# Seven block products for the up pair too, in the last feed-forward block of a decoder step

## The reference

```python
def swiglu(h, w_gate, w_up, w_down):
    return (jax.nn.silu(h @ w_gate) * (h @ w_up)) @ w_down
...
h = modulate(rms_norm(x, norm_ffn2[i]), sh3, sc3)
x = x + 0.5 * gt3[:, None, :] * swiglu(h, ffn2_gate[i], ffn2_up[i], ffn2_down[i])
```

## Time and profile before

| | |
|---|---|
| median of 3 runs | 1440.79 us (1439.36 to 1442.4) |
| the profiled execution | 1442.35 us, span 1440.7 us |
| busy, share of the span | PE 97%, DVE 68%, ACT 37%, POOL 5% |
| granted TensorE clock, mean | 0.990 |
| group 1 of the last feed-forward block, four turns | 1158 to 1244 us of the span |
| group 2, four turns | 1290 to 1377 us |

### The profile page before, as it was taken

How to read it: one execution, slowest core, us unless ns; L and a number is a source line. 1 busy time by engine, 2 the same in 40 slices (tenths; PEclk the granted TensorE clock), 3 DMA queues, 4 the chain that set the end, 5 groups by cost and what they waited for, 6 DMA issues and landing times.

```text
span 1440.7 us, 28804 instructions
## 1 busy us (share of the span) xinstructions
PE 1391.4 (97%) x11790; PEld 1346.0 (93%) x11790; DVE 976.9 (68%) x1731; ACT 539.3 (37%) x797; POOL 77.4 (5%) x118
## 2 busy tenths in 40 slices
PE   6999999999999999999999998999999999999996
PEld 5899999999998999999899897999899999999996
DVE  5446775357546588998998997854554786456745
ACT  5323343224336222524233236422342344224433
POOL 6100000010001000000000000000000000000000
PEclk8999999999999999999999999999999999999998
DMA  9754646455364223213334443626312242223221
GB/s 323 229 180 146 210 150 205 146 166 146 97 206 143 87 88 93 89 60 103 128 123 147 147 156 126 212 89 199 110 41 91 74 134 89 96 81 117 90 87 60
DMA packets 132701, 189.49 MB, mean 132 GB/s; under 512 B 4621, under 2 KB 112545, under 8 KB 132386
## 3 DMA queue, kind: packets, MB, share of 16 engines
q1 hardware_dynamic: 111388, 112.54, 24.7%
q0 software_dynamic: 17136, 66.87, 13.8%
q10 hardware_dynamic: 4070, 8.57, 1.6%
HBM read 173.73 MB, written 15.18 MB: 131 GB/s over the span
## 4 chain that ended last, share of the span: by engine, by line
PE 82%; DVE 11%; ACT 3%; DMA 2%; issue 2%; POOL 0%; DVEq 0%; ACTq 0%; POOLq 0%
PE pu L642 47%; PE pu L817 13%; PE pu L806 11%; PE pu L658 3%; PE pg L679 2%; DVE w_lo L1667 2%; DMA work<-in_w_ada 1%; ACT w_hi L1214 1%; PE pg L1052 1%; DVE d L2087 1%; PE pg L715 1%; PE pg L1116 1%; DMA raw_a<-in_w_ada 1%; DVE w_lo L1956 1%; DVE work L2197 1%
## 5 line engine op out<-in xcount | busy, mean ns | idle before, releaser
L1667 DVE TENSOR_TENSOR w_lo<-raw,w_hi 128x1024 fp32r<-128x1024 f32 x152 | 186.1, 1225 | 259.2 <-ACT w_hi L1214 259.0
L1214 ACT CAST w_hi<-raw 128x1024 fp32r<-128x1024 f32 x152 | 158.8, 1046 | 402.0 <-PE pu L642 360.6
L642 PE MATMUL pu<-h_hi,w_hi 128*128 128x260 f32 x1408 | 288.5, 286 | 5.2 <-DVE w_lo L1667 3.6
L642 PE MATMUL pu<-h_hi,w_lo 128*128 128x260 f32 x1408 | 284.0, 283 | 0.0
L642 PE MATMUL pu<-h_lo,w_hi 128*128 128x260 f32 x1408 | 283.6, 283 | 0.0
L642 PEld LDWEIGHTS pu<-h_hi,w_hi 128*128 128x128 f32 x1408 | 217.5, 189 | 9.0 <-DVE w_lo L1667 5.3
L642 PEld LDWEIGHTS pu<-h_lo,w_hi 128*128 128x128 f32 x1408 | 217.4, 189 | 0.0
L642 PEld LDWEIGHTS pu<-h_hi,w_lo 128*128 128x128 f32 x1408 | 217.4, 189 | 0.0
L2087 DVE SCALAR_TENSOR_TENSOR d<-u,cw,d 128x512 f32<-128x512 f32 x240 | 163.1, 743 | 0.1
L642 PE MATMUL pu<-f_hi,w_hi 128*128 128x260 f32 x704 | 143.1, 284 | 0.9 <-DVE f_lo L2028 0.9
L642 PE MATMUL pu<-f_hi,w_lo 128*128 128x260 f32 x704 | 141.8, 283 | 0.0
(11 more groups left out here) (349 smaller groups left out, 2372.0 us busy)
## 6 DMA issues: line engine op xcount, KB each, us to landing
raw_a<-in_w_ada POOLq DMA_DIRECT2D x30, 1024.0 KB, 7.9
raw<-in_w_in SPq DMA_DIRECT2D x28, 1024.0 KB, 5.2
raw<-in_ffn_up SPq DMA_DIRECT2D x22, 1024.0 KB, 5.3
raw<-in_ffn_gate SPq DMA_DIRECT2D x21, 1024.0 KB, 5.3
raw<-in_ffn_down SPq DMA_DIRECT2D x16, 1024.0 KB, 5.1
gates_d<-sg ACTq DMA_DIRECT2D x24, 260.0 KB, 2.2
raw<-in_ffn_down SPq DMA_DIRECT2D x8, 768.0 KB, 4.4
work<-gates_d POOLq DMA_DIRECT2D x2, 2080.0 KB, 8.6
```

Source lines behind the costliest of these rows:

```text
L642: last = mm(pu[p][:, e, 0:HALF], w[p][:, k, :], m[:, k, e * HALF:(e + 1) * HALF], start=(k == 0 and j == 0), stop=(k == k_tiles - 1 and j ...
L1214: nc.scalar.copy(w_hi[p][:], raw[:, slot, :, p * P:(p + 1) * P]).then_inc(s_hi, 1)
L1667: V.tensor_tensor(w_lo[p][:], raw[:, slot, :, p * P:(p + 1) * P], w_hi[p][:].bitcast(F32), ALU.subtract).then_inc(s_lo, 1)
```

## The change

In the second feed-forward block (`which == 2`), groups 1 and 2, the up pair is made with seven block products too, so a turn has 14 blocks (2 x `PAIR`) and no up units. The first feed-forward block keeps its turns of 11.

- PE: `pairs_of_blocks` issues the gate pair's seven products into the four banks of `pu` and the up pair's seven into the four banks of `pg`. The first down unit waits for all but two hidden tiles ahead of its first matmul, instead of all but one.
- DVE: `pair_turns` makes seven combinations for each pair, the up ones into `lb`, where the gate ones go into `sg`. The sums of weights and the products of gate and up rows leave it, but for the sums of each group's first gate pair, which it still makes during the down units. The low halves of the hidden tiles move to the first positions of the next turn.
- POOL: makes the other sums of weights (four a pair, into `w_sums[:, 1]` for gate and `w_sums[:, 0]` for up) and the products of gate and up rows, in this order in a turn: next gate sums, two products, next up sums. This stands at the end of its list.
- ACT: casts 14 blocks a turn instead of 11, copies a `p1` for each pair, and casts the hidden tiles in the next turn.
- SP: the next up slab waits for the split of the up pair's block P4 and for that pair's sums; the next gate slab waits for the gate pair's sums as well.

```diff
+PAIR = 7
+FFN2_TURN = 2 * TURNS
...
+        def raw_quarter(t, up, m2, k2):
+
+            m2 = m2 if t < FFN2_TURN else 1 - m2
+            return raw[:, up, 4 * k2:4 * k2 + 4, m2 * P:(m2 + 1) * P]
...
+        def sum_of_weights(t, up, k):
+
+            a11, a12, a21, a22 = (raw_quarter(t, up, m2, k2) for m2 in range(2) for k2 in range(2))
+            w = w_sums[:, 1 - up]
+            return ((w[:, 0], a21, a22, ALU.add), (w[:, 1], w[:, 0], a11, ALU.subtract),
+                    (w[:, 2], a11, a21, ALU.subtract), (w[:, 3], a12, w[:, 1], ALU.subtract))[k]
...
                         if it == 0:
                             sp.wait_ge(s_lo, n0 - 2)
                         else:
-                            sp.wait_ge(s_blo, TURN * (t - 1) + P4 + 1)
+                            sp.wait_ge(s_blo, first_block(t - 1) + P4 + 1)
+                            if which == 2:
+                                sp.wait_ge(s_wsum, 4 * pair_no(t - 1) + 4)
...
+                            sp.wait_ge(s_blo, first_block(t - 1) + PAIR + P4 + 1)
+                            sp.wait_ge(s_wsum, 4 * pair_no(t - 1, 1) + 4)
                         sp.dma_start(raw[:, 1], cols(wu, r0 + 256 * it)).then_inc(s_uraw, 16)
...
+            def add_weights(t, up):
+
+                for k in range(4):
+                    pool.wait_ge(s_wsum, 4 * pair_no(t, up) + k)
+                    if k == 0:
+                        pool.wait_ge(s_uraw if up else s_graw, 16 * (t + 1))
+                        if t > FFN2_TURN:
+                            pool.wait_ge(s_blo, first_block(t) if up else first_block(t - 1) + P3 + 1)
+                    out, a, b, op = sum_of_weights(t, up, k)
+                    nc.gpsimd.tensor_tensor(out, a, b, op).then_inc(s_wsum, 1)
+
+            def hidden(t, k):
+
+                pool.wait_ge(s_sg, 2 * t + k + 1)
+                pool.wait_ge((s_c2, s_c12)[k], pair_no(t, 1) + 1)
+                nc.gpsimd.tensor_tensor(lb[:, 1 - k, :], lb[:, 1 - k, :], sg[:, 1 - k, :], ALU.mult).then_inc(s_um, 1)
+
+            for g in (1, 2):
+                for it, t in turns(2, g):
+                    if it == 0:
+                        add_weights(t, 1)
+                    if it + 1 < TURNS:
+                        add_weights(t + 1, 0)
+                    hidden(t, 0)
+                    hidden(t, 1)
+                    if it + 1 < TURNS:
+                        add_weights(t + 1, 1)
...
+                for it, t in turns(2, g):
+                    for up in range(2):
+                        q, j = pair_no(t, up), first_block(t) + PAIR * up
+                        a0, a1, b0, b1 = (pg[:, b, 0:HALF] if up else pu[b // 2][:, b % 2, 0:HALF] for b in range(4))
...
+                        product(j + P1, a0, h_block(h_hi, 0, 0), h_block(h_lo, 0, 0))
+                        product(j + P2, a1, h_block(h_hi, 1, 0), h_block(h_lo, 1, 0))
...
+                        product(j + P6, b0, t_hi[:, 1], t_lo[:, 1])
+                        product(j + P5, b1, t_hi[:, 0], t_lo[:, 0])
+                        pe.wait_ge(s_p1, q + 1)
+                        product(j + P7, a0, t_hi[:, 2], t_lo[:, 2])
+                        pe.wait_ge(s_c11, q + 1)
+                        product(j + P4, a1, t_hi[:, 3], t_lo[:, 3])
+                        pe.wait_ge(s_u2, q + 1)
+                        product(j + P3, b0, h_block(h_hi, 1, 1), h_block(h_lo, 1, 1))
...
+                for it, t in turns(2, g):
+                    for pos in range(2 * PAIR):
+                        up, q = divmod(pos, PAIR)
+                        n = pair_no(t, up) + 1
...
+                        dve.wait_ge(s_bd, first_block(t) + pos + 1)
+                        if q == P2:
+                            dve.wait_ge(s_p1, n)
+                            if not up and t > FFN2_TURN:
+                                dve.wait_ge(s_um, 2 * t)
+                            V.tensor_tensor(r0[:, 0:HALF], p1, bank[1], ALU.add).then_inc(s_c11, 1)
...
+                        if pos + 4 < 2 * PAIR:
+                            block_lo(it, t, pos + 4)
+                        elif it + 1 < TURNS:
+                            block_lo(it + 1, t + 1, pos + 4 - 2 * PAIR)
+                        elif pos in (2 * PAIR - 3, 2 * PAIR - 1):
+                            k = (pos - 2 * PAIR + 3) // 2
+                            split_lo(Lin(at[f"down2_{g}"] + k), k, 0)
+                        if it and pos in (1, 2):
+                            low(t - 1, pos - 1)
+                low(t, 0)
+                low(t, 1)
```

More of the change, by code:

```diff
@@ L223, in decoder_step @@
         sg = sb("sg", [P, 4, N])
-        p1, u2, v2, u3 = (sg[:, 2 + j // 2, j % 2 * HALF:(j % 2 + 1) * HALF] for j in range(4))
+        parts = tuple(tuple(t[:, 2 + j // 2, j % 2 * HALF:(j % 2 + 1) * HALF] for j in range(4)) for t in (sg, lb))
+        p1, u2, v2, u3 = parts[0]
         mod = sb("mod", [P, NADA, 10])
@@ L900, in ffn @@
                     if g:
-                        sums_of_blocks(which, g)
+                        if which == 1:
+                            sums_of_blocks(which, g)
+                        else:
+                            pairs_of_blocks(g)
+                            end = pair_no(list(turns(2, g))[-1][1]) + 1
                     n0 = at[f"up{which}_0"]
@@ L930, in ffn @@
                         for c in range(4):
[L931 to L932 removed]
+                            if g and c < 2 and which == 1:
+                                pe.wait_ge(s_um, 2 * TURNS * g - 1 + c)
+                            if g and c < 2 and which == 2:
+                                pe.wait_ge((s_u3, s_v2)[c], end)
+                                pe.wait_ge((s_c2, s_c12)[c], end)
                             unit(Lin(at[f"down{which}_{g}"] + c, 4, i), c % 2, f_hi, f_lo, GROUPS[g],
[L934 removed]
+                                 ready=(s_a, a0, GROUPS[g] - (2 if which == 2 and g else 1)) if c == 0 else None)
                             ada_part(c, ADA_DOWN[g], i)
@@ L1395, in ffn @@
                 for g in range(3):
-                    if g:
+                    if g and which == 1:
                         gate_turns(which, g, ada_part)
+                    if g and which == 2:
+                        pair_turns(g)
                     n0 = at[f"down{which}_{g}"]
@@ L1937, in add_weights @@
             def add_weights(t, k):
[L1940 to L1943, removed]
+                out, a, b, op = sum_of_weights(t, 0, k)
                 if k == 0:
                     dve.wait_ge(s_graw, 16 * (t + 1))
-                dve.wait_ge(s_wsum, 4 * t + k)
+                dve.wait_ge(s_wsum, 4 * pair_no(t) + k)
                 V.tensor_tensor(out, a, b, op).then_inc(s_wsum, 1)
             def block_lo(it, t, pos):
[L1951 to L1954, removed]
+                j = first_block(t) + pos
+                src, s, v = block_source(t, pos)
+                dve.wait_ge(s, v)
                 dve.wait_ge(s_bhi, j + 1)
@@ L2034, in ffn @@
                 for g in range(3):
-                    if g:
+                    if g and which == 1:
                         gate_turns(which, g, a0 + sum(GROUPS[:g]), ada_part)
+                    if g and which == 2:
+                        pair_turns(g, a0 + sum(GROUPS[:g]))
                     n0 = at[f"down{which}_{g}"]
```

103 lines of the change are left out of this document (90 added, 13 removed).

## The result

The changed kernel takes 1451.07 us (median of 5 runs, 1448.63 to 1455.89) against 1440.79 us before: ratio 1.0074, 95% interval 1.0059 to 1.0088. It is 10.3 us slower, where 3.3 us less was forecast, and it lies 2 us above the range. The profiled execution has a span of 1452.4 us against 1440.7; some 1 us of the difference stands there before the turns of the second feed-forward block begin.

A forecast was written before the change was run, and what follows sets the result against it. TensorE, busy 97% with matmuls end to end, was taken as the bound. Matmuls -11.3 us plus SBUF read port waits +8.0 us gave -3.3 us: 1437.5 us from 1440.79, range of 8 in 10 1430 to 1449.

The forecast's parts named there:

- Matmuls, 11.3 us removed: On PE, the up pair goes from 96 to 84 matmuls, 1.41 us less in each of 8 turns.
- VectorE and ACT by time alone cost nothing: In a 20.16 us turn, VectorE's 14.6 us and ACT's some 12 us of work fit, costing nothing.
- GpSimd's operation, 1.15 us of which 1.05 reads: Each two-input sum or product on POOL over 512 elements takes 1.15 us, 1.05 of it reading SBUF.
- 5 us for each 0.1 us: Some 50 POOL operations lie in turns without reserve, so 0.1 us more reading each costs 5 us.
- What the turns taken cost, 8.0 us: SBUF read port, shared by POOL and two-SBUF-input DVE operations: PE waits 4.0 us a group, 8.0 us in two.
- The first turn fits: In each group's first turn the port's demand, 19.7 us, fits the turn, so PE waits for nothing.
- The last turn, 0.5 us: At its start six POOL operations against seven low halves take 10.5 us, block 7 due at 10.1: 0.5 us counted.
- Moved waits at nothing: Waits for POOL's products and sums, and at a group's end, cost nothing, between 0 and 1 us a group.
- Rival 2: The SBUF read port takes more than the matmuls gave: 1.24 us a read, 6.2 us slower, 1447 us; chance 0.30.
- Rival 1: The SBUF read port is no bound: PE waits less than 1 us in all, 1430.3 us; chance 0.22.

The follow-up runs named there:

- e1: The changed kernel with every two-input GpSimd operation replaced by two memsets, about as slow but reading nothing from SBUF: 1429.79 us, ratio 0.9925.
- f1: The changed kernel with only the up sums replaced by constants on GpSimd; gate sums and products still read SBUF: 1431.67 us, ratio 0.9928.
- f2: The changed kernel with only the gate sums replaced by constants on GpSimd; up sums and products still read SBUF: 1443.8 us, ratio 1.0009.
- f3: The complete changed kernel with VectorE's two low halves of hidden tiles moved from positions 1 and 2 of the next turn to 7 and 10: 1443.2 us.
- e3: The changed kernel with GpSimd's up sums in a group's first turn held until TensorE has ended that turn's product P6: 1450.83 us, ratio 1.0070.
- w1: The complete changed kernel with up sums made by VectorE instead of GpSimd and hidden low halves at positions 7 and 10: 1439.54 us, ratio 0.9987.
- w2: w1 with ScalarE's casts of hidden tiles at positions 4 and 5 instead of 0 and 1, and both their low halves at 7: 1433.53 us.

## Why the prediction was wrong

1. *Matmuls, 11.3 us removed:* right. e1 is 10.7 us below the kernel before, measured beside it (1440.46), with all matmuls of the change, and pieces of 84 take 10.08 us.
2. *VectorE and ACT by time alone cost nothing:* right (e1).
3. *GpSimd's operation, 1.15 us of which 1.05 reads:* a little low. Alone it takes 1.29 us; 1.70 us a pair less VectorE's 0.60 leaves 1.10 us of reading, 1.15 if one goes by the ends in the timeline. By the prediction's own 5 us for each 0.1 us that is 2.5 to 5 us of the 13.6 missing. The estimate from the page GPSIMD Engine Reference (Performance versus the Vector engine) of the Trainium skill, 1.1 us for 512 elements, hit the reading time and not the operation.
4. *What the turns taken cost, 8.0 us:* the step that failed. For the second and third turn it summed the port's demand over a turn and set it against the turn, which gave 1.75 us of wait. That lets what is free late in a turn pay for what is wanted early. It can't: a weight block can be made at most three products ahead, so VectorE's reserve is 2.9 us, whatever idle time comes later. Six reads in a row are 10.2 us in which VectorE passes six operations; TensorE wants seven blocks in that time, and two hidden low halves stood in front of them. By that sum neither f1 nor f2 waits in any turn, and their demand in the second and third turn is the same; yet they differ by 12 us. f3, with the demand unchanged, won 8 us by moving 2 x 0.60 us of work. Measured: 21.4 us of waits, not 8.0; the second and third turns lost 2.8 to 4.5 us each. One thing stays open: f3's second and third turns still lose 2.4 and 2.7 us in group 1, 1.1 and 2.7 in group 2, and the prediction's sum with 1.15 us a read gives 2.7 (10 x 1.15 + 9.6 + 1.8 - 20.16). So the sum may well hold as a lower limit, with the row on top of it; no run tries that.
5. *The first turn fits:* nearly right in group 1 (0.5 us), wrong in group 2. There GpSimd had no loads to finish and began at 1295.69, while VectorE made the first blocks, which have no lead: 3.4 us. The prediction looked at GpSimd's start in group 1 alone. e3 shows that taking this away does not shorten the whole.
6. *The last turn, 0.5 us:* 1.8 us in each group, the same row as in the others. Here the prediction did set the row against a due time, and the way was right; but it counted seven low halves and left out the two hidden ones in front of them. With nine, 6 x 1.05 + 9 x 0.60 = 11.7 us against 10.1, its own working gives 1.6.
7. *Moved waits at nothing:* the down units after each group took 0.3 us longer, inside the bound. The wait of ACT for the products did cost where the row was gone, in w1 (4.5 us with w2's other move); in the change ACT waited 4.5 us for them in all, and how much of that reached TensorE has not been tried apart.

Rival 2 named the sign and the port, at 1447 us, 4 us short. Its number is near by luck in part: it took 1.24 us a read, and at the 1.10 to 1.15 measured its own price gives -0.8 to +1.7 us; what is missing is the row against the lead. Rival 1 is refuted as it was put: GpSimd's reads do bind. The Trainium skill's rule (SBUF — State Buffer, Who interferes with whom) agrees with the trace in three points: a VectorE operation with two SBUF inputs waits for GpSimd's (1.45 to 1.78 us instead of 0.69), one with a PSUM input doesn't (0.41), and a GpSimd operation that only writes doesn't hold it up (e1, 0.69).

## What to carry to other kernels

Moving an operation with two SBUF inputs from VectorE to GpSimd took 0.60 us from VectorE's time and 1.10 to 1.15 us from its access here, so look first whether VectorE reads PSUM or has time to spare at that place; keep such reads few in a row: six in a row cost time (f2), six with four of them late none (f1). When two engines share something, don't stop at the sum of their demands against a whole period: set each row of them against the reserve that stands ahead of it, and look for the place with none, the start of a stage. Work that nobody waits for should stand in a list where the reserve is full, not at the first place where its input is ready.

## What was not expected of the hardware

That the two engines take turns was expected. How strict the turns are was not: 1.70 us a pair, with neither engine twice in succession in the rows read while both had work, so that VectorE passes one operation of two SBUF inputs each 1.70 us where it passes one each 0.60 alone. A read of GpSimd that no one uses costs about as much as one that is used: 96 adds of 128x512 cost the kernel before 27 us, 0.28 us each, and the change's 56 sums and 16 products 21.4 us, 0.30 each. These are means over rows and no price of a read: in f1 40 such reads cost nothing.
